# Three weight tiles of each expert land in extra slots and ScalarE copies them to the ring

## The reference, cut to what matters

```python
logits = ht @ w_router + b_router            # 256 tokens, 32 experts
top_val, top_idx = lax.top_k(logits, 4)
gates = softmax(top_val)
# for each expert e, over its tokens:
hg = x @ w_gu[e] + b_gu[e]                   # 1024 -> 2 x 1024
x_glu = minimum(hg[:, :1024], 7.0)
x_lin = clip(hg[:, 1024:], -7.0, 7.0)
y = (x_glu * sigmoid(1.702 * x_glu) * (x_lin + 1.0)) @ w_down[e] + b_down[e]
# each token: the sum of its four experts' y, each times its gate
```

## Time and profile before

| what | value |
|---|---|
| median of 3 runs | 2350.08 us (2345.67 to 2351.53) |
| profiled execution, its own time | 2346.73 us |
| its span, first to last instruction | 2344.7 us |
| mean granted clock of TensorE | 0.991 |
| PE, DVE, ACT, POOL busy | 95%, 33%, 16%, 13% of the span |
| bytes moved by DMA | 602.75 MB, 257 GB/s over the span |
| chain that ended last | PE 81%, DMA 8%, DVE 4%, SP's queue 3%, ACT 2% |

### The profile page before, as it was taken

The page is one execution under the profiler, slowest core; times in us unless marked ns, Lnnn a source line. Parts: engine busy times, 40 slices in busy tenths (PEclk is TensorE's granted clock), DMA queues, the critical chain, the costliest instruction groups (busy, mean ns, idle before and its releaser), DMA issues.

```text
span 2344.7 us, 33909 instructions
## 1 busy us (share of the span) xinstructions
PE 2232.5 (95%) x11106; PEld 1275.5 (54%) x11107; DVE 782.5 (33%) x1691; ACT 385.8 (16%) x849; POOL 313.3 (13%) x2286
## 2 busy tenths in 40 slices
PE   7999999999999989999999899988899999998997
PEld 3564458888544678998888533322233333332333
DVE  1134545555660334874124322111122112121112
ACT  3222221111001412220234300000000001000001
POOL 0000000000000000000000033322233333332332
PEclk9999999999999999999999899999999999999999
DMA  9711342222683606558851399999987989999896
GB/s 380 255 61 54 109 139 78 87 90 86 193 279 128 211 1 198 163 168 293 271 176 62 135 415 422 422 422 422 422 352 285 422 342 423 422 422 422 358 422 272
DMA packets 196205, 602.75 MB, mean 257 GB/s; under 512 B 11042, under 2 KB 128034, under 8 KB 146850
## 3 DMA queue, kind: packets, MB, share of 16 engines
q1 hardware_dynamic: 193728, 599.04, 66.8%
q10 hardware_dynamic: 2402, 2.67, 0.4%
HBM read 600.62 MB, written 1.05 MB: 257 GB/s over the span
## 4 chain that ended last, share of the span: by engine, by line
PE 81%; DMA 8%; DVE 4%; SPq 3%; ACT 2%; issue 1%; POOL 0%; DVEq 0%; POOLq 0%; ACTq 0%
PE bank L363 53%; PE bank L955 26%; DMA wring<-in_w_gu 8%; SPq L2187 3%; DVE big L1535 1%; DVE big L1541 1%; DVE big L1538 1%; PE bank L987 1%; ACT big L1116 1%; ACT hT L1116 1%; DVE wring L1535 0%; DMA tabs<-in_tab 0%; PE bank L980 0%; ACT tmp L1116 0%; DVE tmp L1535 0%
## 5 line engine op out<-in xcount | busy, mean ns | idle before, releaser
L955 PE MATMUL bank<-wring,big 128*64 128x512 f32 x3456 | 777.7, 597 | 52.3 <-DMA wring<-in_w_gu 27.2
L955 PEld LDWEIGHTS bank<-wring,big 128*64 128x64 f32 x3456 | 233.5, 136 | 542.9 <-issue 420.4
L363 PE MATMUL bank<-hT,wring 128*128 128x256 f32 (+2 forms) x1888 | 452.8, 393 | 6.2 <-ACT hT L1116 6.0
L363 PEld LDWEIGHTS bank<-hT,wring 128*128 128x128 f32 x1888 | 319.9, 192 | 122.1 <-issue 81.3
L363 PE MATMUL bank<-big,wring 128*128 128x256 f32 (+1 forms) x1096 | 346.0, 477 | 6.4 <-DVE big L1538 3.5
L2173 POOL COPY big<-hT 128x8 f32 x2240 | 301.6, 197 | 112.1 <-issue 112.1
L363 PEld LDWEIGHTS bank<-big,wring 128*128 128x128 f32 x1096 | 209.7, 192 | 139.4 <-issue 115.8
L2166 POOL TENSOR_TENSOR big<-big 1x1 f32<-1x1 f32 x35 | 6.4, 183 | 1885.2 <-DVE rows L2104 1885.2
L363 PE MATMUL bank<-wring 128*128 128x256 f32 (+1 forms) x1408 | 245.8, 327 | 0.9 <-DVE wring L1535 0.8
L363 PEld LDWEIGHTS bank<-wring 128*128 128x128 f32 x1408 | 216.0, 191 | 20.0 <-DVE wring L1535 1.3
L1116 ACT ACTIVATE big<-bank 128x256 f32<-128x256 f32 (+3 forms) x203 | 87.2, 430 | 787.3 <-PE bank L980 433.2
(11 more groups left out here) (159 smaller groups left out, 1193.9 us busy)
## 6 DMA issues: line engine op xcount, KB each, us to landing
wring<-in_w_gu SPq DMA_DIRECT2D x256, 1024.0 KB, 17.3
wring<-in_w_down SPq DMA_DIRECT2D x128, 1024.0 KB, 17.9
wring<-in_ffn_w_up SPq DMA_DIRECT2D x44, 1024.0 KB, 5.1
wring<-in_mod_w SPq DMA_DIRECT2D x24, 1024.0 KB, 15.3
wring<-in_mod_w SPq DMA_DIRECT2D x48, 512.0 KB, 4.5
wring<-in_ffn_w_down SPq DMA_DIRECT2D x16, 1024.0 KB, 5.2
wring<-in_w_ada SPq DMA_DIRECT2D x16, 1024.0 KB, 5.1
wring<-in_w_in SPq DMA_DIRECT2D x14, 1024.0 KB, 11.9
```

Source lines behind the costliest of these rows:

```text
L363: ins = pe.matmul(o, l, r, start=start, stop=stop, skip_group_check=True)
L955: ins = pe.matmul(o, l, r, start=start, stop=stop, skip_group_check=True)
```

## The change

Three further slots (`STAGE`) are laid over rows 16 to 23 and 0 to 3 of `big`; for this `big` and `wring` become parts of one tensor `mem`. Tiles 0 to 2 (`AHEAD` = 3) of experts 1 to 31 land in these slots, and ScalarE copies them to slots of the ring during `down` of the block before. The source of the copy is a register address: the staged slot if the block is the last of its expert, else the ring's slot itself. The flag for this (`keep`) is a third row of the tables. SP issues the three loads of expert 1 as soon as the residual is ready, and those of expert e + 1 behind the loads of tiles 3 to 11 of expert e. `H2` moves to the free half of `xT`, `XN` becomes `XS`, `SGS`, `OH` and `diag` move.

On PE the bias products move from behind the first tile to behind `scatter`, with their waits in the middle of `scatter`. `turn_act` and `take_act` are done in two halves, in banks 6 and 7. On DVE the one-hot moves into `activate`, behind the first clamp.

```diff
+AHEAD = 3
-        wring = sb("wring", [P, RING, SLOT])
+        mem = sb("mem", [P, 24 * T2 + RING * SLOT])
+        big = mem[:, 0:24 * T2].rearrange("p (a b) -> p a b", b=T2)
+        wring = mem[:, 24 * T2:].rearrange("p (a b) -> p a b", b=SLOT)
-        big = sb("big", [P, 24, T2])
-        H2 = big[:, 0:4, :]...
+        STAGE_AT = [T2 * 16, T2 * 20, 0]
+        STAGE = [mem[:, at:at + SLOT] for at in STAGE_AT]
-        XN = big[:, 20, :]
+        XN = XS
+        def h2(tt, g):
+            return xT[:, 4 * tt + 2 * g:4 * tt + 2 * g + 2, S:T2]
...
-            mm(bk[:, 0:2 * (MAXB + 1)], ones, diag, True, True, fl)
+            mm(bk[:, 0:3 * (MAXB + 1)], ones, diag, True, True, fl)
-            def wslot(s, e):
+            def wslot(s, e, b=None):
                 i, uses, last = places[base + s]
-                pe.wait_ge(w_full[i], e * 16 + 16 * (uses + 1))
+                if s >= AHEAD:
+                    pe.wait_ge(w_full[i], e * 16 + 16 * (uses + 1))
+                elif b is None:
+                    pe.wait_ge(w_full[i], 16 * (uses + 1))
+                else:
+                    pe.wait_ge(G("m_staged"), b * AHEAD + (s + 1 - AHEAD))
-            def turn_act():
-                for c in range(4):
+            def turn_act(hf):
+                for c in (2 * hf, 2 * hf + 1):
                     at = 256 * (c // 2) + c % 2
-                    ins = pe.transpose(bank[6][:, P * c:P * c + P], AV[:, at:at + 255:2], ident)
-                ins.then_inc(G("m_at"), 1)
+                    ins = pe.transpose(bank[6 + c // 2][:, P * c:P * c + P], AV[:, at:at + 255:2], ident)
+                    if c % 2:
+                        ins.then_inc(G("m_at"), 1)
-            def down(e, ss=range(4)):
+            def down(e, n, ss=range(4)):
                 for s in ss:
+                    if s < 2:
+                        pe.wait_ge(G("m_ac"), 2 * n + s - 1)
...
             with pe.Fori(1, nblk) as b:
-                pe.wait_ge(G("m_oh"), b + 1)
-                pe.wait_ge(G("m_lin_in"), b)
                 pe.wait_ge(G("m_xg"), b + 1)
-                gate_up(range(1), e, G("moe_used"))
-                bias()
-                gate_up(range(1, 2), e)
+                gate_up(range(2), e, G("moe_used"), b)
                 pe.wait_ge(G("m_gs"), b)
                 flip(bank[7], SGS.rearrange("p t s -> p (t s)"), 2, G("m_gt"))
-                gate_up(range(2, 8), e)
+                gate_up(range(2, 8), e, None, b)
                 pe.wait_ge(G("m_sgt"), b)
                 token_ids(b + 3, G("moe_used"))
+                def banks_read():
+                    pe.wait_ge(G("m_oh"), b + 2)
+                    pe.wait_ge(G("m_lin_in"), b + 1)
                 pe.wait_ge(G("m_yk"), b)
-                scatter()
+                scatter(None, banks_read)
+                bias()
                 pe.wait_ge(G("m_act"), b + 1)
-                turn_act()
-                pe.wait_ge(G("m_ac"), b + 1)
-                down(e)
+                turn_act(0)
+                pe.wait_ge(G("m_tok"), b + 1)
+                turn_act(1)
+                down(e, b + 1)
...
             def take_act(n):
-                act.wait_ge(G("m_at"), n)
-                A(AC, bank[6][:, :], ACT.Copy).then_inc(G("m_ac"), 1)
+                for hf in range(2):
+                    act.wait_ge(G("m_at"), 2 * n + hf - 1)
+                    A(AC[:, S * hf:S * hf + S], bank[6 + hf][:, S * hf:S * hf + S], ACT.Copy).then_inc(G("m_ac"), 1)
+            def stage(b, nxt, keep):
+                for s in range(AHEAD):
+                    act.wait_ge(G(f"m_stage{s}"), nxt * 16 + 16)
+                act.wait_ge(G("moe_used"), b * RING + AHEAD)
+                A(big[0:1, 14, 304:305], IDS[0:1, 0:1], ACT.Copy)
+                for s in range(AHEAD):
+                    i = places[MOE["slot0"] + s][0]
+                    own = 24 * T2 + SLOT * i
+                    A(wring[:, i, :], mem[:, bass.ds(keep * (own - STAGE_AT[s]) + STAGE_AT[s], SLOT)],
+                      ACT.Copy).then_inc(G("m_staged"), 1)
             with act.Fori(1, nblk) as b:
+                nxt = act.value_load(itab[0:1, 0, bass.ds(b + 1, 1)], ...)
+                keep = act.value_load(itab[0:1, 2, bass.ds(b, 1)], ...)
                 take_g(b)
                 sig(b + 1)
                 take_columns(b + 2)
                 take_act(b + 1)
+                stage(b, nxt, keep)
...
+            for st in range(AHEAD):
+                TS(big[:, 14, 300 + st:301 + st], sm[:, 32:33], 1.0, None, MUL).then_inc(G(f"m_stage{st}"), 16)
+            TS(ends, cum, minus_p, 1.0, ADD, ALU.is_equal).then_inc(G("ends"), 1)
+            dve.wait_ge(G("ends"), 1)
+            link(v.tensor_reduce(col[:, 3:4], ends, AX.X, ADD))
+            link(TS(col[:, 3:4], col[:, 3:4], -1.0, 1.0, MUL, ADD))
+            TS(diag[:, 2 * (MAXB + 1):], C("ident", 0, MAXB + 1), col[:, 3:4], None, MUL)
...
+            v.tensor_copy(itab[:, 2, 0:MAXB], bk[:, 2 * (MAXB + 1):2 * (MAXB + 1) + MAXB])
...
-            def activate(n):
+            def activate(n, e):
                 TS(GL, bank[4][:, :], 7.0, None, ALU.min).then_inc(G("m_glu_in"), 1)
+                one_hot(e)
                 dve.wait_ge(G("m_lin"), n)
...
             for s in range(RING):
                 wait_free(n0 + s)
                 load(n0 + s, expert(s, 0), SLOT)
+            sp.wait_ge(G("x_mixed"), DC)
+            for s in range(AHEAD):
+                sp.dma_start(STAGE[s], expert(s, 1)).then_inc(G(f"m_stage{s}"), 16)
             sp.wait_ge(G("tables"), 1)
-            with sp.Fori(1, NE) as e:
+            with sp.Fori(1, NE - 1) as e:
                 c = sp.value_load(itab[0:1, 1, bass.ds(e - 1, 1)], min_val=0, max_val=MAXB - 2)
-                for s in range(RING):
+                for s in range(AHEAD, RING):
                     sp.wait_ge(G("moe_used"), c * RING + (s + 1))
-                    load(n0 + s, src, SLOT)
+                    load(n0 + s, expert_at(s, e), SLOT)
+                for s in range(AHEAD):
+                    sp.wait_ge(G("m_staged"), c * AHEAD + (s + 1))
+                    sp.dma_start(STAGE[s], expert_at(s, e + 1)).then_inc(G(f"m_stage{s}"), 16)
+            c = sp.value_load(itab[0:1, 1, NE - 2:NE - 1], min_val=0, max_val=MAXB - 2)
+            for s in range(AHEAD, RING):
+                sp.wait_ge(G("moe_used"), c * RING + (s + 1))
+                load(n0 + s, expert(s, NE - 1), SLOT)
```

More of the change, by code:

```diff
@@ L307, in program @@
         le2 = big[:, 14, NE:2 * NE]
-        col = big[:, 14, 2 * NE:2 * NE + 3]
-        diag = big[:, 15, 0:2 * (MAXB + 1)]
+        col = big[:, 14, 2 * NE:2 * NE + 4]
+        ends = big[:, 14, 2 * NE + 8:3 * NE + 8]
+        diag = big[:, 14, 128:128 + 3 * (MAXB + 1)]
         LP = GL[:, 0:S]
+        def h2(tt, g):
+            return xT[:, 4 * tt + 2 * g:4 * tt + 2 * g + 2, S:T2]
         pgain = sm[:, 112:120]
@@ L973, in gather @@
                         last = tt == 1 and i == 1
-                        xmm(halves(bank[7], i), SEL[:, tt, :], H2[:, tt, T2 * i:T2 * i + T2], tt == 0, tt == 1,
+                        xmm(halves(bank[7], i).rearrange("p (a b) -> p a b", b=S), SEL[:, tt, :], h2(tt, i), tt == 0, tt == 1,
                             G("m_rows") if last else inc if (tt == 0 and i == 0) else None)
@@ L1000, in bias, with gate_up @@
                     rows_of = slice(64 * hf, 64 * hf + 64)
-                    xmm(halves(bank[4 + hf], i), OH[rows_of, i, :], BG[rows_of, :], False, False)
-            def gate_up(ts, e, first=None):
+                    xmm(halves(bank[4 + hf], i), OH[rows_of, i, :], BG[rows_of, :], True, False)
+            def gate_up(ts, e, first=None, b=None):
                 for t in ts:
-                    ws = wslot(t, e)
+                    ws = wslot(t, e, b)
                     for q in range(4):
@@ L1026, in down, with scatter @@
                                 (G("m_y") if s == 3 else G("moe_used")) if last else None)
-            def scatter(inc=None):
+            def scatter(inc=None, halfway=None):
                 for c4 in range(4):
+                    if c4 == 2 and halfway:
+                        halfway()
                     for i in range(2):
@@ L1046, in _ @@
             pe.wait_ge(G("m_oh"), 1)
+            bias()
             pe.wait_ge(G("m_xg"), 1)
-            gate_up(range(1), 0)
-            bias()
-            gate_up(range(1, 8), 0)
+            gate_up(range(8), 0)
             gather(2, G("moe_used"))
@@ L1059, in _ @@
             pe.wait_ge(G("m_act"), 1)
[L1060 removed]
+            turn_act(0)
             pe.wait_ge(G("m_rows_out"), 2)
             flip(bank[7], XS, 4, G("m_x"))
[L1063 to L1064 removed]
             pe.wait_ge(G("m_xg"), 2)
+            turn_act(1)
+            pe.wait_ge(G("m_lin_in"), 1)
+            pe.wait_ge(G("m_oh"), 2)
+            bias()
+            down(0, 1, range(2))
             token_ids(3, None)
[L1067 removed]
+            down(0, 1, range(2, 4))
```

(18 more changed lines are left out.)

26 lines of the change are left out of this document (11 added, 15 removed).

## The result

| | before | after |
|---|---|---|
| median | 2348.16 us (2345.67 to 2351.53, 15 runs) | 2354.95 us (2350.68 to 2362.87, 15 runs) |
| ratio after to before | | 1.003, 95% interval 1.0023 to 1.0038 |
| span of the profiled execution | 2344.7 us | 2353.1 us |
| mean granted clock of TensorE | 0.991 | 0.981 |

The change makes the kernel about 0.3% slower. The forecast, 2344.8, was 0.2% faster: the time went the other way. It lies inside the range given, at the slow end, which the rivals had made that wide and not the forecast itself. In the new listing PE's products stand on L968, ScalarE's operations on L1139, the loads of ring slots on L2235 and those of the extra slots on L2302; ring and slots are one tensor, `mem`.

What follows compares the result with a forecast made beforehand. Single-block experts run at the loads' rate; PE gains time only at four two-block experts, where loads stop. Start, stops and last blocks together gave -5.3 us from 2350.08: 2344.8 us, range 2333 to 2357.

Steps and rivals of the forecast that it cites:

- the block: Mixture of experts, one 64-token block at PE's rate: 26.26 us falls to 25.6, saving 0.65, bounds 0.35 and 0.75.
- the restarts behind experts 12 and 14: PE sets the restart of loads at expert 14; three shorter blocks between the two restarts give -1.95 us.
- the copies and the wait: ScalarE copies of 128x2048 take 1.85 us each, hidden; at the loads' rate PE waits once per block, about 4.2 us.
- that the wait costs only PE's lateness: At the loads' rate a block ends 5.4 us behind the next expert's last landing, now 2.95; no clock cost in the sum.
- a rival with a chance of 0.22: TensorE's clock falls in the new wait: 3.4 us more at experts 12 and 27, 2348 to 2352 us; chance 0.22.
- the work around these gaps is denser than at 817.5: Argument against the clock falling: the trace's 3.5 us gap at 817.5, followed by half clock, has less dense work around it.
- at most every other block falls: Argument against the clock falling: a block delayed by it leaves a gap of only 0.8 us behind it.
- the start: Stage start: tables +1.1 us, first refill waiting for tile 3 +5.25, three tiles of expert 1 loaded early -7.46.
- DMA doesn't starve: At the loads' rate, nine tiles are still queued when SP's wait for the expert's last tile ends, so loads continue.
- The stop behind expert 12: Restart 12.8 us behind the last landing, less 7.46 staged: a stop of 5.4 us for 4.8, +0.6.
- Behind expert 18: Five shorter blocks would give -3.25 us, but the stop, about 7.7 now, can't go under 5.4: -2.3.
- The slots: Extra slots buy less than three tiles: first refill waits 5.25 us of PE work more, for 7.46 us of loads made.

Runs made afterwards that it cites:

- the kernel with the old order: Changed kernel with its staged loads and copies, but bias, transposes, one-hot and ScalarE's copy ordered as in the kernel before: 2361.36 us, ratio 1.0051.
- the one with the lump alone: Kernel before plus one PE wait for tile 3 ahead of tile 0, without extra slots or copies: 2358.62 us, ratio 1.0044.
- the order alone: Changed kernel without staging (`AHEAD` = 0), its new order on PE, ACT and DVE kept: 2343.15 us, ratio 0.9973 to the kernel before.
- the slots tile by tile: Changed kernel, ScalarE waiting for and copying each staged tile singly: three slots 2342.71 us (0.9978), two 2343.44 (0.9974), one 2341.38 (0.9977).

## Why the prediction was wrong

**Right: the block.** 25.51 us for 25.6, a saving of 0.75 for 0.65 (bounds 0.35 to 0.75). The copy of the halves leaves 0.23 of wait, the transposes and the bias are as costed, and the waits moved into the scatter cost nothing. Between the restarts behind experts 12 and 14 that gave -2.24 for -1.95 (-2.5 from landing to landing).

**Right: the copies and the wait.** 1.90 us a copy for 1.85; one wait a block, ended by ScalarE, of 4.0 us for 4.2 in six blocks and of 1.1 to 2.7 in ten; restarts at the four places.

**Wrong: that the wait costs only PE's lateness.** This is the step of the mechanism that failed. The forecast counted what the wait of 4.2 us in one piece makes PE later, and put nothing for the clock; its fall stood beside the sum as a rival with a chance of 0.22. It is what happened. The argument against it, that the work around these gaps is denser than at 817.5, didn't hold: all six waits of 4.0 us brought the fall. The other remark, that at most every other block falls, held up to expert 18 and not behind it, where the falls at 2060.9, 2091.6 and 2122.4 are three blocks in a row. The first 16 products of experts 12, 18 and 27:

```profile
1691.28 5.35 PE L968 MATMUL bank<-mem 128*64 128x512 f32 x16 [4.01 <-ACT mem L1139]
...
1899.61 5.35 PE L968 MATMUL bank<-mem 128*64 128x512 f32 x16 [2.33 <-ACT mem L1139]
...
2180.77 5.13 PE L968 MATMUL bank<-mem 128*64 128x512 f32 x16 [4.02 <-ACT mem L1139]
```

They take 3.74 us at full clock, so PE came 1.6, 1.6 and 1.4 us later, 4.6 in all. The lateness itself was sized about right: less the clock, the restart stands 13.3 us behind the last landing, for 12.8. The clock doesn't decide the sign alone: 8.4 less 4.6 is still slower. The rule of the Trainium skill, TensorE: Matmul & The Clock Gate, Part 1: The HAM clock gate, that PE drops to half rate after an idle stretch, is borne out here, by the earlier trace rows and by the 0.50 behind the wait at 1508. Not every wait of 3.3 us brought it: five of seven did in the kernel with the old order, six of eight in the one with the lump alone.

**Wrong: the rival's own size.** It gave 2348 to 2352 and the time is 2354.95. It priced the fall at 3.4 us each at experts 12 and 27; it came at expert 18 too, at 1.4 to 1.6 each, and longer in block 0 (2.3, below). That the two sums, 6.8 and 6.9, are nearly one is luck. What the rival lacked is in the next two steps.

**Wrong: the start, +3.7 for -1.1.** The first refill is 8.5 us later (1353.82; before it was 1345.28), where 5.25 + 1.1 were counted. The stretches of block 0 in the changed kernel:

```profile
1327.10:1341.00 13.90, 8.78 (x44) 5.66 (x44) 7.76 (x50) 1.90 (x4) 0.00 (x0) 0.50 0.02 7
1341.00:1347.50 6.50, 5.81 (x22) 1.70 (x20) 1.23 (x3) 1.88 (x2) 0.00 (x0) 0.50 0.00 0
1347.50:1354.00 6.50, 6.50 (x34) 2.17 (x32) 0.00 (x0) 0.00 (x0) 0.00 (x0) 1.00 0.00 0
```

```profile
1342.63 1.11 PE L993 MATMUL bank<-tabs,mem 128*128 128x128 f32 x4 [0.69 <-ACT mem L1139]
1343.68 1.99 PE L968 MATMUL bank<-tmp,mem 64*64 64x512 f32 x8
1345.59 14.90 PE L968 MATMUL bank<-mem 128*64 128x512 f32 x64
```

Half clock lasts to 1347.5; in the kernel before it ended at 1341.0. From start to start, the transposes take 1.05 us (0.66 before) and the bias 1.91 (1.02 in the earlier trace rows), and the first tiles lose half of 1347.5 less 1345.59: 0.4 + 0.9 + 1.0 = 2.3. And the bias, 1.0, stands ahead of tile 0 in block 0 too, which the forecast didn't count there, while 0.8 of wait ahead of tile 0 went. The tables cost what was forecast: PE's wait for them went from 0.98 to 2.07. That is 5.25 + 1.1 + 2.3 + 1.0 - 0.8 = 8.9, for 8.5 measured. Some 2.5 us more than before are gaps between landings, behind tiles 7 to 9 and behind the first staged tile: 8.5 - 7.46 + 2.5 = 3.5, for 3.7.

**Wrong: "DMA doesn't starve".** True at the loads' rate, which is what that step spoke of; behind a restart only five tiles are free, and tile 8 lands 1.7 to 1.9 us late behind experts 12, 14 and 18. The stop behind expert 12 was to add +0.6. The restart is 2.1 us later than forecast (14.9 behind the last landing, not 12.8; 1.6 of it clock), and between the restart and its last landing expert 13 loses 1.1 us more to gaps than in the kernel before: 0.6 + 2.1 + 1.1 = 3.8, for 3.7. Behind expert 18 it was -2.3 and is +1.8: the same floor, 2.1 higher, and 2.1 more lost between the landings.

**The difference in one sum.** From -5.3 to +8.4 is 13.7 us: clock 4.6 + 2.3, gaps in the loads 2.5 + 1.1 + 2.1, bias ahead of tile 0 less the wait that went 0.2, the rest of the late restarts 2 x 0.5, less 0.6 of the block: 13.2. So two terms that the forecast had at nothing carry it, the clock with 6.9 and the gaps in the loads with 5.7. Why a load that is issued late comes that late stays open (last section).

**The slots.** That they are worth less than three tiles was seen. That they are worth nothing measurable even with the clock kept up was not: the refill hangs on the first tile that isn't staged, so each slot gives 2.49 us and takes 1.75 back; the dip takes part of the rest, and block 0, some 2.3 us longer with slots, the other.

Four versions beat both kernels: the order alone, and the slots tile by tile with one, two or three of them, all at 0.997 to 0.998. The simplest, the order alone, is the one to keep.

## What to carry to other kernels

Total waiting time is not the whole price of waits: the same 28 us in pieces of up to 4.0 us and in pieces of up to 1.3 us ended 12 us apart: 4.6 of them because the clock fell behind the long ones, the others because the work behind each began later. Where several loads are waited for ahead of one piece of work, wait for each just ahead of its own part. And before a buffer is deepened, ask which event then lets the next load start, and which one the load after that.

## What was not expected of the hardware

- Waits of 2.3 to 2.7 us brought the fall in four of eight cases, and one of 2.00 us did in the kernel with the old order, in work that otherwise ran at 1.00; two of seven waits of 3.3 us there did not. Waits up to 1.4 us never did, in 986 us of the stage of each version tile by tile. What decides between the cases isn't shown.
- In block 0 the half clock lasted 20.5 us in all five profiles with staged loads and 13.7 us in the other four. PE's longest wait for the tables just ahead was 1.96 to 2.08 us in the former and 0.98 to 1.83 in the latter. Whether the one causes the other was not tried.
- A load issued 3.0 to 3.3 us before the queue ran out of bytes still landed 1.3 to 2.0 us late, though the first load behind a stop lands 4.7 us after its issue, of which its 1 MB takes 2.49. Through the dip the rate falls to some 290 GB/s and not to 0. Why a queue with bytes left takes up the next load so slowly stays open.
